# Moving four of the modulation's weight blocks from the retrieval to the attention

## The reference, cut to what matters

```python
out = lax.map(block, hb_all)            # retrieval: u = expert_u[idx], sum of wts * expert_v[idx]
...
mod = (jax.nn.silu(c) @ ada_w + ada_b)[:, None, :]       # ada_w is 1024 x 6144
sh1, sc1, gt1, sh2, sc2, gt2 = jnp.split(mod, 6, axis=-1)
h = rmsnorm_2(x, norm1_g) * (1.0 + sc1) + sh1
(aq, ak, av, iq, ik, iw, bq, bf, bi, bg, cq, ck, cv, cg, ga, gb, gc) = split_cols(h @ w_in)
o_a = dsa_attention(...)
...
x = x + gt1 * (merged @ w_out)
h2 = rmsnorm_2(x, norm2_g) * (1.0 + sc2) + sh2
x = x + gt2 * hier_moe(h2, ...)
```

## Time and profile before

| what | us |
|---|---|
| runs, median (lowest, highest) | 2303.38 (2300.12, 2304.31), 3 runs |
| profiled execution, its own time | 2300.97 |
| its span | 2299.2 |
| TensorE busy / vector engine busy | 1934.7 / 1526.6 |
| ScalarE busy / GpSimd busy | 945.1 / 648.5 |
| chain that ended last: TensorE / DMA / vector engine | 57% / 19% / 16% |
| of it the gathers of the retrieval (`in_expert_uv`) | 18% |

### The profile page before, as it was taken

The page is one execution under the profiler, slowest core; times in us unless marked ns, Lnnn a source line. Parts: engine busy times, 40 slices in busy tenths (PEclk is TensorE's granted clock), DMA queues, the critical chain, the costliest instruction groups (busy, mean ns, idle before and its releaser), DMA issues.

```text
span 2299.2 us, 23970 instructions
## 1 busy us (share of the span) xinstructions
PE 1934.7 (84%) x9004; PEld 1412.1 (61%) x9004; DVE 1526.6 (66%) x2331; ACT 945.1 (41%) x1343; POOL 648.5 (28%) x409
## 2 busy tenths in 40 slices
PE   6898667777767777689998888998969999999996
PEld 6785522222222222378987778778658887878784
DVE  7962766767777765434349734443359999999996
ACT  4333311121122211244343423354147887877774
POOL 4423434444434433237433432333120000000000
PEclk9999889999999989999999989999979999999998
DMA  8664589999989999554343225443429999999993
GB/s 321 253 257 164 212 358 422 421 421 421 414 352 421 421 419 409 238 165 156 128 176 97 86 94 189 141 177 129 131 98 361 365 365 343 364 352 364 364 353 124
DMA packets 92258, 634.90 MB, mean 276 GB/s; under 512 B 10940, under 2 KB 13628, under 8 KB 16488
## 3 DMA queue, kind: packets, MB, share of 16 engines
q1 hardware_dynamic: 48096, 350.25, 41.2%
q0 software_dynamic: 36864, 268.45, 28.3%
q10 hardware_dynamic: 7176, 14.60, 1.9%
HBM read 632.17 MB, written 1.09 MB: 275 GB/s over the span
## 4 chain that ended last, share of the span: by engine, by line
PE 57%; DMA 19%; DVE 16%; issue 3%; ACT 3%; ACTq 1%; POOL 0%; DVEq 0%; POOLq 0%
DMA t<-in_expert_uv,t 18%; PE ps L965 5%; PE ps L967 5%; PE ps L966 5%; PE ps L508 3%; PE ps L666 3%; PE ps L510 3%; PE ps L512 3%; PE ps L542 3%; PE ps L667 3%; PE ps L681 3%; PE ps L994 3%; PE ps L995 2%; PE ps L996 2%; PE ps L555 2%
## 5 line engine op out<-in xcount | busy, mean ns | idle before, releaser
L158 ACT ACTIVATE t<-ring 128x1024 fp32r<-128x1024 f32 x588 | 617.2, 1060 | 360.8 <-PE ps L967 74.4
L166 DVE TENSOR_TENSOR t<-ring,t 128x1024 fp32r<-128x1024 f32 x450 | 565.8, 1283 | 161.4 <-ACT t L158 147.8
L166 POOL TENSOR_TENSOR t<-ring,t 128x1024 fp32r<-128x1024 f32 x138 | 357.5, 2602 | 529.6 <-ACT t L158 529.4
L666 PE MATMUL ps<-t 128*128 128x512 f32 x512 | 284.0, 637 | 202.0 <-ACT t L1240 202.0
L1753 DVE CUSTOM_DVE_ANT_0 t<-t 128x1024 f32<-128x1024 f32 x256 | 312.9, 1225 | 197.8 <-DMA t<-in_expert_uv,t 196.0
L2292 POOL DMA_INDIRECT t<-in_expert_uv,t x256 | 281.3, 1099 | 410.6 <-PE ps L667 386.5
L666 PEld LDWEIGHTS ps<-t 128*128 128x128 f32 x512 | 90.9, 196 | 370.6 <-ACT t L1240 265.8
L667 PE MATMUL ps<-t 128*128 128x512 f32 x512 | 269.6, 609 | 0.0
L1214 ACT ACTIVATE t<-t 128x2 f32<-128x2 f32 x128 | 26.0, 203 | 540.6 <-DVE t L1753 540.3
L965 PE MATMUL ps<-t 128*128 128x512 f32 x512 | 206.4, 403 | 2.1 <-DVE t L166 1.3
L967 PE MATMUL ps<-t 128*128 128x512 f32 x512 | 202.0, 395 | 0.0
(11 more groups left out here) (333 smaller groups left out, 2640.7 us busy)
## 6 DMA issues: line engine op xcount, KB each, us to landing
ring<-in_w_in SPq DMA_DIRECT2D x82, 1024.0 KB, 4.9
ring<-in_eg SPq DMA_DIRECT2D x64, 1024.0 KB, 7.2
ring<-in_eu SPq DMA_DIRECT2D x64, 1024.0 KB, 7.0
ring<-in_ed SPq DMA_DIRECT2D x64, 1024.0 KB, 7.2
ring<-in_ada_w SPq DMA_DIRECT2D x24, 1024.0 KB, 7.1
ring<-in_w_out SPq DMA_DIRECT2D x8, 1024.0 KB, 4.9
ring<-in_w_q SPq DMA_DIRECT2D x8, 1024.0 KB, 4.9
ring<-in_w_branch_c SPq DMA_DIRECT2D x8, 1024.0 KB, 4.8
```

Source lines behind the costliest of these rows:

```text
L158: e.activation(p.hi, p.view, ACT.Copy).then_inc(self.w.hi, 1)
L166: e.tensor_tensor(p.lo, p.view, p.hi.bitcast(F32), ALU.subtract).then_inc(self.w.lo[eng], 1)
L666: e.matmul(sums[tt][0], s.diag[col % 4], v[:, 1024:1536], start=first, stop=last)
```

## The change

The last four modulation blocks (eight chunks of 1 MB) leave the retrieval. In the ring's order they now stand in pairs behind the two units of `av` and the two of the gate: `av` 5, block 8, `av` 6, block 9, gate 27, block 10, gate 28, block 11, then `wa` and unit 9. Their steps are poured after each of the sixteen parts 20 to 35, two at a time, on the vector engine, TensorE and ScalarE. On the vector engine block 8 stands behind the logits and ahead of the first softmax, block 9 between the softmaxes, blocks 10 and 11 behind the second. The rows that need block 8 and 9 (`mod_d[4]`) or reuse their buffer are loaded and combined in the recurrence, and ScalarE waits for the last stores at the end of the attention. The bias is loaded at the attention's start.

```diff
@@ lay_out @@
-    s.ada = [m.w.ada_pair(a["ada_w_2"][n]) for n in range(8, 12)]
...
-    t_("V", 4), t_("G", 0, 1, 2, 3), n_("G", 5, 6), t_("G", 27), t_("GV", 28)
+    t_("V", 4), t_("G", 0, 1, 2, 3)
+    s.ada = []
+    for n, unit in enumerate((lambda: n_("G", 5), lambda: n_("G", 6), lambda: t_("G", 27), lambda: t_("GV", 28))):
+        unit()
+        s.ada.append(m.w.ada_pair(a["ada_w_2"][8 + n]))
@@ pe_retrieval (dve_retrieval and act_retrieval lose the same lines) @@
-    ada = pe_ada(m, e, s, 8, 12, (m.d_adab.sem, 16))
...
-        if 200 <= c0 < 236:
-            pour(ada)
@@ pe_attention @@
+    ada = pe_ada(m, e, s, 8, 12, (m.d_adab.sem, 16))
     for n in range(2):
-        run(pe_rows(m, e, s.sp, ("av", n), s.hT))
+        for _ in pe_rows(m, e, s.sp, ("av", n), s.hT):
+            pour(ada)
     for n in range(2):
-        run(pe_cols(m, e, s.sp, ("gate2", "a", n), s.hT))
+        for _ in pe_cols(m, e, s.sp, ("gate2", "a", n), s.hT):
+            pour(ada)
+    pour(ada, 100)
@@ act_retrieval, act_attention @@
-    m.d_adab.up(e.dma_start(s.adab[0:12, :], ...))
+    m.d_adab.up(e.dma_start(s.adab[0:12, :], ...))     # now behind the load of t.wsm
...
-    act_row(m, e, m.d_row1, 1, m.mod_d[4, :])
-    e.wait_ge(*m.rows_ready.turn("act"))
-    act_row(m, e, m.d_row3, 3, a["final_norm_g_2"])
...
+    ada = act_ada(m, e, s, 8, 12)
     for tt in range(2):
-        run(act_rows(m, e, s.sp, ("av", tt), t.av, tt))
+        for _ in act_rows(m, e, s.sp, ("av", tt), t.av, tt):
+            pour(ada)
         e.wait_ge(*m.logits.turn("act"))
         m.att_exp.up(e.activation(t.Ls[tt], t.Ls[tt], ACT.Exp))
     for n in range(2):
-        run(act_cols(m, e, s.sp, ("gate2", "a", n), s.sg, n, ACT.Sigmoid))
+        for _ in act_cols(m, e, s.sp, ("gate2", "a", n), s.sg, n, ACT.Sigmoid):
+            pour(ada)
+    pour(ada, 100)
     for tt in range(2):
         for k in range(tt + 1):
             act_out(m, e, ("pT", tt, k, 1), t.PT[tt][k][:, 4:8, :], n=4)
...
+    e.wait_ge(m.d_mod0.sem, 96)
+    e.wait_ge(m.d_mod1.sem, 96)
@@ dve_attention @@
-    e.wait_ge(m.d_row1.sem, 32)
-    e.wait_ge(m.d_row3.sem, 32)
-    m.rows_ready.up(e.scalar_tensor_tensor(out=m.grow[1], ...))
...
-    for tt in range(2):
-        takes(e, s.sp, 4)
+    ada = dve_ada(m, e, s, 8, 12)
+    for tt in range(2):
+        for _ in range(4):
+            s.sp.take(e, "V")
+            pour(ada)
         n = 128 * (tt + 1)
...
-    takes(e, s.sp, 8)
+    for _ in range(8):
+        s.sp.take(e, "V")
+        pour(ada)
+    pour(ada, 100)
```

More of the change, by code:

```diff
@@ L351, in lay_out @@
     s.diag = [ar(scope, 128) for _ in range(4)]
-    s.adab = ar(scope, 512)
-    s.msum, s.modr = ([ar(scope, 512) for _ in range(2)] for _ in range(2))
     scope.close()
@@ L395, in lay_out @@
     at.m8, at.mx = ar(inner, 8), ar(inner, 48)
+    s.adab = ar(inner, 512)
+    s.msum = [ar(inner, 512) for _ in range(2)]
     first = ExitStack()
@@ L401, in lay_out @@
     at.av = r3(ar(inner, 2048), 2)
+    s.modr = [ar(inner, 512) for _ in range(2)]
     inner.close()
@@ L1203, in act_retrieval @@
     e.wait_ge(m.d_rr.sem, 16)
-    m.d_adab.up(e.dma_start(s.adab[0:12, :], a["ada_b_2"].rearrange("o (n c) -> (o n) c", n=12)), 16)
-    ada = act_ada(m, e, s, 8, 12)
     act_row(m, e, m.d_row0, 0, a["norm1_g_2"][0, :])
@@ L1247, in act_attention @@
     m.d_att.up(e.dma_start(t.wsm, a["w_small"]), 16)
+    m.d_adab.up(e.dma_start(s.adab[0:12, :], a["ada_b_2"].rearrange("o (n c) -> (o n) c", n=12)), 16)
     m.d_att.up(e.dma_start(t.flip, a["cst"][:, C_OH + 512:C_OH + 640]), 16)
@@ L1270, in act_attention @@
             b.emptied(e.activation(r3(t.Ls[tt], 8)[:, 2 * hp:2 * hp + 2, :], r3(b.ap(key), 2)[:, :, 0:n], ACT.Relu), key)
-    e.wait_ge(m.d_mod0.sem, 96)
-    e.wait_ge(m.d_mod1.sem, 96)
     act_row(m, e, m.d_row0, 0, m.mod_d[2, :])
-    act_row(m, e, m.d_row1, 1, m.mod_d[4, :])
     act_row(m, e, m.d_row2, 2, m.mod_d[3, :])
@@ L1307, in act_recurrence @@
     run(act_cols(m, e, s.sp, ("bf", 1), b3(h.bk), 1, ACT.Sigmoid))
+    act_row(m, e, m.d_row1, 1, m.mod_d[4, :])
     run(act_cols(m, e, s.sp, ("bq", 0), b3(h.bq), 0))
@@ L1337, in act_recurrence @@
     act_out(m, e, ("cross", 1), b3(h.accx)[:, 4:8, :], n=4)
+    e.wait_ge(*m.rows_ready.turn("act"))
+    act_row(m, e, m.d_row3, 3, a["final_norm_g_2"])
     e.wait_ge(*b.taken(("bg", 1, 1)))
@@ L1742, in dve_retrieval @@
     run(dve_softmax(m, e, 0, 1))
-    e.wait_ge(m.d_adab.sem, 16)
-    ada = dve_ada(m, e, s, 8, 12)
     e.wait_ge(m.d_row0.sem, 16)
@@ L1832, in dve_attention @@
         m.v(e.tensor_tensor(sc2, sc2, sc, ALU.is_equal))
-    takes(e, s.sp, 4)
-    e.wait_ge(m.d_row1.sem, 32)
-    e.wait_ge(m.d_row3.sem, 32)
-    m.rows_ready.up(e.scalar_tensor_tensor(out=m.grow[1], in0=m.grow[1], scalar=1.0, in1=m.grow[3],
-                                           op0=ALU.add, op1=ALU.mult))
-    takes(e, s.sp, 8)
+    takes(e, s.sp, 12)
     e.wait_ge(*b.taken(("flip", 1, 3)))
@@ L1950, in dve_recurrence @@
         kept(6, 6, 5, hf)
+    e.wait_ge(m.d_row1.sem, 32)
+    e.wait_ge(m.d_row3.sem, 32)
+    m.rows_ready.up(e.scalar_tensor_tensor(out=m.grow[1], in0=m.grow[1], scalar=1.0, in1=m.grow[3],
+                                           op0=ALU.add, op1=ALU.mult))
     B4 = h.bb.rearrange("p (h c t) -> p h c t", h=8, c=4)
```

## The result

The change makes the kernel slower: 2313.86 us (median of 6 runs, 2308.36 to 2317.30) against 2302.86 (median of 6). The ratio is 1.0047, 95% interval 1.0036 to 1.0059, so +11.0 us on the medians. The profiled execution has a span of 2313.0 us, 13.8 more than before. The prediction was 2312, with 2299 to 2322, and "slower" at 75%.

The account below looks back on a forecast made before the run. It took the retrieval's end as bound by DMA bandwidth and the attention by TensorE, with in-order queues deciding. -22.6 + 30.8 + 2.0 = +10.2 us on 2300.97 gives 2311.2 (2313.6 by the median); forecast 2312, range 2299 to 2322.

Parts of the forecast that it names:

- retrieval: Retrieval's end: 8.4 MB fewer loads beside the gathers let 49 columns go at the undisturbed 2.485 us; -22.6 us.
- vector engine's chain to block 11's first half: Attention: blocks 8 to 10, both softmaxes, two low halves and block 11's first chunk, from the logits on; 42.4 us.
- load of part 36's chunk: Attention: load issued once block 11's first half frees its slot, with ScalarE waiting for it; 5.0 us.
- from there to pT's eviction: Attention: parts 36 and 37, four last steps, a second load, part 38, last gate eviction, two stores; 16.1 us.
- less the same stretch before: Attention: the kernel before's time from the logits at 1089.6 to pT's eviction at 1122.3, subtracted; -32.7 us.
- the clock after the stand: Start of pv and the merge: TensorE at 1.2 instead of 2.4 GHz after standing; +2.0 us, bounds 0 and 4.
- recurrence and all behind: Stages behind the attention: unchanged, 0 us.
- The loop of waits: Attention: late-freed slots and in-order queues hold loads, ScalarE's evictions and pT, whose evictions begin 30.8 us later.
- The sum by that rule: Attention: seven GpSimd low halves of 2.75 us fully block the vector engine; chain 48.9 instead of 42.4 us.
- The row product in the recurrence: End of the recurrence's levels: the moved 1.2 us vector-engine product hides in 6.66 us of idling, costing nothing.

Follow-up runs that it names:

- e7: The kernel before, with seven of the eight steps of blocks 8 to 11 working on 64 of 512 columns; 2302.03 us.
- e2: The changed kernel without modulation blocks 8 to 11 at all (no loads, steps, sums or stores); 2279.76 us.
- e1: The changed kernel, the vector engine making four steps after each of the gate's first four takes instead of two after each of eight; 2304.87 us.
- e5: The changed kernel with all four blocks ahead of av, their steps poured after parts 4 to 19 (query and key); 2290.73 us, 2290.97 when run again.
- e6: The changed kernel, with seven of the eight steps of blocks 8 to 11 working on 64 of 512 columns; 2310.02 us.
- e4: The changed kernel, blocks 8 and 9 poured after parts 12 to 19, blocks 10 and 11 in the gate ahead of its second unit, four steps a turn; 2295.92 us.
- e10: e1 with the low halves of parts 33 and 35 made by GpSimd instead of the vector engine; 2302.76 us.

## Why the prediction was right, step by step

The mechanism, its places and its sign were those of the prediction. Its sum against the profile, every row in us:

| term | predicted | measured | from |
|---|---|---|---|
| retrieval | -22.6 | -21.6 | last gather 943.70 and 922.08 |
| last gather to the end of the logits | 0 | +1.3 | 145.9 and 147.2 (147.5 in e7, with the same instructions as before) |
| vector engine's chain to block 11's first half | 42.4 | 45.2 | 1069.27 to 1114.45 |
| load of part 36's chunk | 5.0 | 8.4 | 1114.47 to 1122.89 |
| from there to pT's eviction | 16.1 | 15.8 | 1122.89 to 1138.67 |
| less the same stretch before | -32.7 | -32.7 | 1089.6 to 1122.3 |
| the clock after the stand | +2.0 | -0.5 | 1138.67 to 1147.27, 9.15 before |
| recurrence and all behind | 0 | -2.0 | what is left of 13.8 |
| sum | +10.2 | +13.8 | rounded |

- *The retrieval's gain* was right, and for the stated reason as far as e7 shows it by excluding the steps; e2 has it too. It is 1 us less than forecast because the 49 columns took 123.1 us and not the 121.8 of the undisturbed pace.
- *The loop of waits* was right in each link, and e1 shows one of them by itself: taking the last four steps out from behind part 37 brings pT 6.8 us and the merge 4.6 us earlier. e5 shows the whole: without the late slots nothing is lost behind the logits.
- *The vector engine's chain* was 2.8 us short, and that is what is left of two errors. Blocks 8 and 9 took 22.1 us against my 16.7: L1557 took 1324 ns on average in them, and 1.65 us in block 9, against my 1.24. All the rest took 23.1 against 25.7.

```profile
L1557 DVE SCALAR_TENSOR_TENSOR t<-ring,st,t 128x512 f32<-128x512 f32 x14 | 18.5, 1324 | 0.6
```

I weighed the rule of the Trainium skill ("SBUF — State Buffer", "Who interferes with whom") that a vector instruction with two SBUF inputs and a GpSimd instruction that reads SBUF exclude each other. The trace agrees with the mechanism: the steps of this run take 0.76 us or, where one of GpSimd's stands in the way, about 2.7 us, with nothing much between. The sum by that rule, 48.9 us for the chain, was 3.7 too high, mine 2.8 too low. It had added seven times 2.75 us. Seven instructions of the blocks were indeed held up, but by 2.0 to 2.1 us each (five L1557 of 2.74 to 2.79 us and two L1554 of 2.6), 14.3 in all.

- *The load* was mis-sized: 5.0 us holds for one load alone. Here three `wa` chunks had been issued 3.9 us ahead, and it took 8.4; in e6, behind four, 10.65. An estimate from the bytes ahead fits: 3 x 1.05 MB at the 421 GB/s of the stretches above are 7.5 us, less the 3.9 already gone 3.6 (measured 3.4 more than the 5.0); with four and 4.8 us gone, 5.2 (measured 5.6). It fits three more runs that it wasn't made from: with one chunk 0.4 us ahead it gives 7.1 us (6.96 in e1 and e4), with three, the first 2.8 us ahead, 9.7 (9.5 in e10). The prediction named the links of the loop, but not that loads are issued in bunches.
- *The clock.* The granted clock did fall to half in the stand (0.50 at 1122 to 1137 us, 1.00 from 1138 on). But what TensorE made at that clock, the last sum, pT and the first eight products of pv, ran while the chain was at the second load and on ScalarE. When pT's eviction let it go on, eight products took 1.13 us again instead of 1.98. The 0.5 us below zero come mostly from those first eight products, which before stood behind the eviction. The term should have been 0 because the slow work was hidden, not because the clock didn't fall.

```profile
1136.19 1.98 PE L770 MATMUL ps<-t 128*128 128x128 f32 x8
1139.41 1.13 PE L770 MATMUL ps<-t 128*128 128x128 f32 x8 [1.24 <-ACT t L1051]
```

- *The row product in the recurrence* was hidden, as forecast: it runs at 1312.77 us, and behind it the engine still idles 3.36 us for ScalarE (6.66 before). The stages behind the merge are 2 us shorter, not longer: the second merge begins 14.6 us later than before, the first 15.8, and the rest of the difference comes in small steps behind. That is no more than this part varies from run to run.

```profile
1312.77 1.21 DVE L1956 SCALAR_TENSOR_TENSOR g<-g 128x1024 f32<-128x1024 f32 x1
...
1321.89 1.22 DVE L1970 TENSOR_TENSOR t<-t 128x1024 f32<-128x1024 f32 x1 [3.36 <-ACT t L1340]
```

The two sizes that were too small (+2.8, +3.4) and the two that were too large (2.5 and 2.0) nearly cancel; that the median came out 2 us from the number is partly luck. The sum by terms is 13.8 us against the 11.0 of the medians, since the profiled execution of the kernel before lay 1.9 us below its median and that of the changed kernel 1.0 above. What was not foreseen at all is how far the price depends on the order: the same blocks in the same stage cost 33 us as the change has them, 25 with one number changed (e1), and 11 in e5 by the medians (37, 31 and 14 from the last gather to the merge in the traces). The prediction's text said only what the placement does, not that another one would turn the sign.

## What to carry to other kernels

- When work moves into a stage that has room for it by its busy shares, don't sum its instructions; walk each in-order queue. Ask for every buffer it takes: which instruction frees it, what stands ahead of that instruction on its engine, and what load is next in line for it, with all loads behind that one.
- Put such work where its engine idles and its buffers come free early, even if that is far from where its result is used. Here the vector engine's idle stretches under query and key took all four blocks, and with that +11 us became -11.
- A load's time is that of its place in the queue: if loads go out in bunches, count the bytes ahead of it.
- Before a median is explained, see in the trace where the time lies. Here two experiments had part of their difference in stages that they didn't touch.

## What the runs showed of the hardware that was not expected

- A 1 MB load issued right behind three or four others landed after 8.4 and 10.65 us, right behind one after 6.96 (e1), alone after 4.9.
- A 128x512 multiply-add on the vector engine takes 0.75 us alone and about 2.7 us each time a subtraction of GpSimd is in its way; even the 128x512 product with a scalar, 0.48 us alone, took 2.62 (1069.19 us). Cutting the step to 64 columns brought only its own share down, to 0.28 us where GpSimd made no subtractions (e7).
